# A mixture-of-experts layer on one Trainium2 core: expert rows added into a token table by scatters, in place of a result table that is gathered at the end

## What is computed

```
h  = rmsnorm(x1)                                   # h2 in the kernel
pc = softmax(h @ w_rc)       # 4 groups            -> best group g, its probability p
pf = softmax(fine logits of group g)               # 8 experts -> the best two, top_w
w  = top_w / sum(top_w) * p                        # two mixing weights per token
y  = x1 + sum over the 2 experts:  w * ((silu(h @ gate) * (h @ up)) @ w_down)
```

## Time and profile before

| | |
|---|---|
| median of 3 runs | 1653.49 us (1650.79 to 1655.81) |
| the profiled execution: its time / its span | 1649.68 / 1647.9 us |
| busy in the span: PE, DVE, ACT, POOL | 1531.3, 735.6, 398.5, 202.2 us |
| router stage | about 1048 to 1217 us |
| expert stage | 1220 to 1597 us |
| tail | 1597 to 1648 us |

### The profile page before, as it was taken

The page is one execution under the profiler, slowest core; times in us unless marked ns, Lnnn a source line. Parts: engine busy times, 40 slices in busy tenths (PEclk is TensorE's granted clock), DMA queues, the critical chain, the costliest instruction groups (busy, mean ns, idle before and its releaser), DMA issues.

```text
span 1647.9 us, 16294 instructions
## 1 busy us (share of the span) xinstructions
PE 1531.3 (93%) x6131; PEld 951.5 (58%) x6131; DVE 735.6 (45%) x1311; ACT 398.5 (24%) x662; POOL 202.2 (12%) x224
## 2 busy tenths in 40 slices
PE   8999999989987989999999999999949999999976
PEld 6676666645655657556989766555524444444432
DVE  4667876022342433797677453245433212111116
ACT  3211101015466564331313220011111111111113
POOL 0000010000000000154378200000110000000004
PEclk9999999999998999999999999999969999999997
DMA  5274873513231012325221424432368999999938
GB/s 165 80 109 138 244 231 95 139 75 83 77 89 39 25 30 91 87 68 154 75 71 29 151 67 177 158 122 102 131 201 308 368 366 374 365 369 373 365 130 309
DMA packets 232261, 273.25 MB, mean 166 GB/s; under 512 B 62516, under 2 KB 167336, under 8 KB 231920
## 3 DMA queue, kind: packets, MB, share of 16 engines
q1 hardware_dynamic: 204628, 203.54, 39.9%
q10 hardware_dynamic: 18140, 34.48, 5.5%
q0 software_dynamic: 9408, 34.08, 5.4%
HBM read 188.83 MB, written 83.24 MB: 165 GB/s over the span
## 4 chain that ended last, share of the span: by engine, by line
PE 78%; DVE 7%; ACT 6%; issue 4%; POOL 2%; DMA 2%; ACTq 0%; POOLq 0%; SPq 0%; DVEq 0%
PE P L694 24%; PE P L1143 12%; PE P L1094 7%; PE P L1050 7%; PE P L1127 6%; PE P L851 2%; PE P L875 2%; PE P L1114 2%; POOL arena L602 1%; DVE arena L1449 1%; PE P L826 1%; POOL arena L661 1%; DVE arena L1451 1%; PE P L1074 1%; PE P L720 1%
## 5 line engine op out<-in xcount | busy, mean ns | idle before, releaser
L694 PE MATMUL P<-arena 128*128 128x352 f32 (+1 forms) x1728 | 538.5, 467 | 7.8 <-ACT arena L2133 6.5
L694 PEld LDWEIGHTS P<-arena 128*128 128x128 f32 (+1 forms) x1728 | 324.5, 191 | 195.1 <-issue 37.5
L1143 PE MATMUL P<-arena 128*128 128x512 f32 x512 | 227.9, 598 | 0.8 <-ACT arena L2234 0.8
L1143 PEld LDWEIGHTS P<-arena 128*128 128x128 f32 x512 | 95.9, 192 | 110.0 <-issue 110.0
L1094 PE MATMUL P<-arena 128*128 128x512 f32 (+1 forms) x288 | 130.6, 603 | 1.9 <-DVEq L1627 1.9
L1771 DVE COPY arena<-P 128x512 f32<-128x512 f32 x32 | 22.1, 692 | 215.8 <-PE P L1114 215.8
L1050 PE MATMUL P<-arena 128*128 128x352 f32 x384 | 115.1, 459 | 1.1 <-DMA arena<-y_d 1.1
L1127 PE MATMUL P<-arena 128*128 128x512 f32 x256 | 115.3, 593 | 0.9 <-DVE arena L1811 0.9
L1050 PEld LDWEIGHTS P<-arena 128*128 128x128 f32 x384 | 72.9, 190 | 41.6 <-issue 1.2
L1094 PEld LDWEIGHTS P<-arena 128*128 128x128 f32 (+1 forms) x288 | 50.8, 183 | 63.4 <-issue 60.9
L602 POOL TENSOR_TENSOR arena<-arena,N 64x256 f32<-64x256 f32 x96 | 81.1, 845 | 49.1 <-ACT arena L2155 27.8
(11 more groups left out here) (405 smaller groups left out, 1889.4 us busy)
## 6 DMA issues: line engine op xcount, KB each, us to landing
arena<-in_w_expert_up_dram SPq DMA_DIRECT2D x32, 2048.0 KB, 12.8
arena<-in_w_expert_down_dram SPq DMA_DIRECT2D x32, 1024.0 KB, 7.4
arena<-in_w_in_dram SPq DMA_DIRECT2D x36, 512.0 KB, 4.1
x_d<-zero SPq DMA_DIRECT2D x4, 4096.0 KB, 20.2
arena<-x_d POOLq DMA_DIRECT2D x32, 512.0 KB, 5.6
y_d<-arena ACTq DMA_DIRECT2D x32, 512.0 KB, 7.7
gate_d<-arena ACTq DMA_DIRECT2D x16, 528.0 KB, 4.9
arena<-gate_d SPq DMA_DIRECT2D x24, 352.0 KB, 3.2
```

The source lines that it names most:

```text
L694: m = pe.matmul(P[0:p, b + j, 0:TBK], w[:, k, 0:p], hT[:, k, TBK * j:TBK * j + TBK], start=f, stop=l)
L1143: m = pe.matmul(P[:, i % 2, :], xgT[i % 2][:, k, :], WU[i % NWE][:, k, :], start=k == 0, stop=k == KD - 1)
```

## The change

- `y_d` goes, with the eight DMAs that clear it. In its place is `acc_d`, a DRAM table with one row for each token. SP writes `x1` of each token tile into it during the router stage.
- The mixing weights are worked out tile by tile in the router stage. `gaps` (two DVE instructions) comes behind `choose`; `exponentials` (one ACT instruction) behind the root of the next tile, with a table load to Exp ahead and one back to Sqrt behind it; `mixing_weights` (four DVE instructions) behind `h2` of the next tile.
- Before, `idx_d`, the table from slot to token, was filled only where further tiles run. Now `owner_rows` scatters a pair (token, weight) for every slot in use, 18 scatters in the router stage; ACT loads the table back once (`owners_loaded`), PE transposes it (`owners_transposed`) and DVE copies it out (`owners_of_rows`), all before the result of tile 0 is copied. Slots without a token hold 8192, which lies past the bound of the scatters, so they are skipped.
- ACT and DVE multiply by the weight `wc` as they copy the result out of PSUM. POOL then adds the rows of the tile into `acc_d` with one indirect DMA (`add_rows`) that has `compute_op=ALU.add`. A scatter waits for the one before it to land, since two tiles can hold the same token.
- In the tail SP waits for the last scatters, skips the four conditional groups, and loads nine tiles from `acc_d` into `x1`; ACT and DVE take the norm, and SP stores. The gathers, `combine`, and PE's sums are gone.

```
+        acc_d = dram("acc_d", (NT, D))
...
             for i in range(TT_):
                 n = rows(i)
                 pool.wait_ge(s_h2, i + 1)
...
+                if i >= 1:
+                    pool.wait_ge(s_mw, i)
+                    owner_rows(i - 1, pos_i, E * 128)
...
+            def add_rows(i):
+                pool.wait_ge(s_yoa, i + 1)
+                pool.wait_ge(s_yov, i + 1)
+                if i >= 1:
+                    pool.wait_ge(s_yod[(i - 1) % 2], 16 * ((i - 1) // 2 + 1))
+                pool.indirect_dma_start(acc_d, bass.IndirectOffsetOnAxis(idx_i[:, i:i + 1], 0), yo[i % 2], None,
+                                        bounds_check=NT - 1, oob_is_err=False, compute_op=ALU.add
+                                        ).then_inc(s_yod[i % 2], 16)
...
                 for i in range(lo, hi):
+                    tile_rows(i)
+                    if i == 1:
+                        pool.wait_ge(s_mw, TT_)
+                        owner_rows(TT_ - 1, pos_i, E * 128)
...
+                    if i >= lo + 4:
+                        add_rows(i - 4)
+                for i in range(hi - 4, hi):
+                    add_rows(i)
...
+            def owners_transposed(loaded):                                  # PE, behind gathered(2)
+                pe.wait_ge(s_idn, loaded)
+                bank = bank6()
+                for a in range(2):
+                    m = pe.transpose(bank[:, NTILE * a:NTILE * a + NTILE], idx_n[:, :, a], ident[0:NTILE, 0:NTILE])
+                m.then_inc(s_6, 1)
...
+            def gaps(i):                                                    # DVE
+                c = slice(i, i + 1)
+                link(dve.tensor_tensor(ex5[:, i, 0:NG], lg[:, i, :], m4[:, c].broadcast_to([128, NG]), ALU.subtract))
+                dve.tensor_tensor(ex5[:, i, NG:NG + 1], m8[1][:, c], m8[0][:, c], ALU.subtract).then_inc(s_ex, 1)
+                dve.wait_ge(s_ex, i + 1)
+
+            def mixing_weights(i):
+                c = slice(i, i + 1)
+                second = ex5[:, i, NG:NG + 1]
+                dve.wait_ge(s_exa, i + 1)
+                link(dve.tensor_reduce(p4[:, c], ex5[:, i, 0:NG], AX, ALU.add))
+                link(dve.scalar_tensor_tensor(p4[:, c], second, 1.0, p4[:, c], ALU.add, ALU.mult))
+                link(dve.reciprocal(tokw[:, i, 0, 1:2], p4[:, c]))
+                dve.tensor_tensor(tokw[:, i, 1, 1:2], tokw[:, i, 0, 1:2], second, ALU.mult).then_inc(s_mw, 1)
+                dve.wait_ge(s_mw, i + 1)
...
-                dve.tensor_copy(yo[i % 2][:, 512:1024], P[:, 3 + 2 * (i % 2), :]).then_inc(s_yov, 1)
+                dve.tensor_scalar(yo[i % 2][:, 512:1024], P[:, 3 + 2 * (i % 2), :], wc[:, i:i + 1], None,
+                                  ALU.mult).then_inc(s_yov, 1)
...
-                act.activation(yo[i % 2][:, 0:512], P[:, 2 + 2 * (i % 2), :], ACT.Copy).then_inc(s_yoa, 1)
-                act.wait_ge(s_yoa, i + 1)
-                act.wait_ge(s_yov, i + 1)
-                act.dma_start(y_d[128 * i:128 * i + 128, :], yo[i % 2]).then_inc(s_yod[i % 2], 16)
+                act.wait_ge(s_idx, 2 if i < E else 4)
+                act.activation(yo[i % 2][:, 0:512], P[:, 2 + 2 * (i % 2), :], ACT.Copy, scale=wc[:, i:i + 1]).then_inc(s_yoa, 1)
...
                 if i >= 1:
                     sp.wait_ge(s_h2, i)
                     sp.dma_start(h2_d[128 * i - 128:128 * i, :], h2[(i - 1) % 2]).then_inc(s_h2s[(i - 1) % 2], 16)
+                    sp.wait_ge(s_zid, 16)
+                    sp.dma_start(acc_d[128 * i - 128:128 * i, :], x1[:, i - 1, :]).then_inc(s_zid, 16)
...
+                for b in range(2):
+                    sp.wait_ge(s_yod[b], 16 * hi // 2)
...
+            for i in range(TT_):
+                n = rows(i)
+                sp.dma_start(x1[0:n, i, :], acc_d[128 * i:128 * i + n, :]).then_inc(s_land[i], 16)
```

More of the change, by code:

```diff
@@ L258, in hybrid_step @@
         WRr = at(q + 2048, KD, 36)
-        yg = [at(i * D, D) for i in range(2 * TT_)]
         xr = [at(q + 2336 + i * D, D) for i in range(2)]
@@ L1640, in _ @@
             link(dve.tensor_copy(tokf, tok_i[:]))
+            for j in range(2):
+                link(dve.tensor_copy(tokw[:, :, j, 0], tokf))
             link(dve.tensor_copy(tilef, des_i[:]))
```

221 lines of the change are left out of this document (88 added, 133 removed).

## The result

The changed kernel takes 1657.88 us (median of 20 runs, 1651.3 to 1661.37) against 1650.61 us (20 runs, 1647.62 to 1655.81) for the kernel before on the same chip. The ratio is 1.004, 95% interval 1.0028 to 1.0052: slower by 0.4%. The forecast was 1640 us and faster. The value lies inside the wide range of 1630 to 1670 us, which took in a rival, and outside the forecast's own of 1631 to 1647; the direction was wrong. The time base was off too: the forecast built on a median of 3 runs, 1653.49 us, which is 2.9 us above the median of 20.

What follows compares the result with a forecast made beforehand. PE was taken to bound router and expert stages, no engine the tail. 1.5 + 2.5 + 0.8 + 0 - 17.4 = -12.6 us took the profiled 1649.68 to 1637.1; predicted 1640 us, own range 1631 to 1647, wide range 1630 to 1670.

Steps and rivals of the forecast that it cites:

- Expert stage: Adding scatter in place of each tile's store: 1.2 us per engine and tile against 1.3, PE stays the bound, 0 us.
- own upper bound: Expert stage: two packets a row and all 66 rows on half the engines, 2.3 us per engine and tile.
- rival in the mild form: Expert stage: adding scatters overload the DMA engines, 20 us of PE waits, 1660 us; chance of the whole rival 0.20.
- The reserve: Expert stage: up matrices land 13.0 us after issue and are used after 22.8, so weights have some 9.8 us in hand.
- Serial scatters: Rival, expert stage: adding scatters over 10.4 us make POOL fall behind each tile; at 14 us about 1740; chance 0.08.
- Tail: From the last copy out of PSUM to the end: 33 us against 50.6, -17.4 us (bounds -24 and -8).
- Router stage and handover: Router: added DVE work stalls PE in 7 tiles, +1.5 us; handover to the experts: DVE and POOL work, +2.5 us.
- Index table: Before the expert stage: loading hidden, but PE's two transposes wait for DVE to free bank 6 and run, +0.8 us.
- Clears: The eight clears of `y_d` lie beside PE-bound projection work and are worth nothing.

Runs made afterwards that it cites:

- c_spread: The changed kernel with each expert's first 64 rows dealt to even partitions, the others to odd ones, by two more VectorE instructions a router tile; 1648.77 us, ratio 0.9978.
- c_blocks: The changed kernel with an expert's rows dealt to partitions 0 to 31, then 64 to 95, 32 to 63, 96 to 127; 1656.91 us, expert stage 372.5 us.
- c_fours: The changed kernel with an expert's first 64 rows dealt to the first four partitions of every eight, the others to the rest; 1666.84 us, expert stage 385.0 us.
- c_all128: The changed kernel with each tile's unused slots added too, into 128 spare rows of a larger table, so 128 adding rows a tile; 1648.04 us, ratio 0.9970.
- a3_clears: The changed kernel with the eight 1 MB clears put back at the same places, into a table nobody reads; 1655.43 us, ratio 1.0021.
- b_tail: The changed kernel with the tail's nine loads issued by GpSimd instead of SyncE and a buffer for each output; 1656.66 us, ratio 1.0033.
- e_ctrl: c_all128 with only the scatter's bound set so that the spare rows are skipped again; 1658.89 us, ratio 1.0064.
- a1_plain: The changed kernel with scatters that overwrite token rows instead of adding (adding left out, so no candidate); 1641.98 us, ratio 0.9936.
- a5_skipped: The changed kernel with a scatter bound that lets only token row 0 through (adding the others left out, so no candidate); 1643.46 us, ratio 0.9951.

## Why the prediction was wrong

**Expert stage, the step that failed.** "I take 1.2 (66/16 x 0.28), two packets evenly spread ... no change in demand, and PE stays the bound, 0 us". It cost +11.9 us. The price of two packets was right, 0.33 us a row against 2 x 0.16 (it is one record of twice the length). The even spread was wrong. The rows lie on half of the engines, 8 on each, so by an estimate 2.6 us of such an engine's time a tile (8 x 0.33), double the store's 1.3. c_spread, c_blocks and c_fours show it by moving rows alone. The forecast's own upper bound had 2.3 us, and its rival in the mild form 1660 us; measured were 1657.88. The mechanism of that rival is the one that came, but the nearness of its time is in part luck: it had 20 us of waits and the full gain of the tail, where 11.9 us more stage came with 5.6 us less gain. What would show it was named too: PE waits for weight loads. The forecast also knew that the used slots are the first of each tile. Against it stood only that 419 GB/s had been seen, and that is a sum over all 16 engines, which says nothing of one half of them.

**The reserve.** The rival let PE wait when the 9.8 us in hand were used up, and so it was: PE is still busy to 99.5% from 1300 to 1400 us, and most of the waits come behind that. What it did not foresee is that eight rows on every engine (c_all128) use up the reserve so much more slowly, 15.6 to 17.5 us over the stage, than eight rows on half of them. So the busiest engine's load alone does not decide, and this part stays open.

**Serial scatters.** This rival did not come about. An adding scatter of the changed kernel lands in 6.1 to 10.1 us, under the 10.4 from which GpSimd would fall behind, though over the 9 that the forecast had named; GpSimd waits for the one before only once, for 5.7 us at the last tile.

```profile
DMA to landing us min/median/max: 6.1/9.5/10.1
```

**Tail, a term that was mis-sized.** -17.4 us forecast. The mean over the changed kernel and the three others with its tail and its scatters (a3_clears 36.9, b_tail 37.0, e_ctrl 38.3) is 37.4 us, over the two profiles of before 49.2: -11.8. The part behind the first load was well forecast, 25 us against 26.0. The part ahead of it was not: "The last scatter needs 5 us ... and the one before has landed by then". The one before landed only at about 1623.9, the last started at 1624.73, 3.2 us behind E, and took some 6.4 us more. So the load went out at E + 11.5, not at E + 8. And 1.4 us of the 17.4 were in the 50.6 us of one profile.

**Router stage and handover.** +4.0 forecast, measured 180.4 against 176.2, so +4.2; over the seven profiles of the change with nothing added in that stage 178.6 to 180.6 against 174.3 and 176.2. Between profiles with the same mean granted clock in the stage the difference is as large: 180.4 against 176.2 us at 0.93, and 178.6 (a3_clears) against 174.3 at 0.94. The handover's parts were not told apart by a run. There was no drain behind a table load, as the forecast took from the earlier trace rows (changed kernel, ScalarE's timeline):

```profile
1194.91 1.28 ACT L2206 ACT_TABLE_LOAD   x1
1196.20 0.21 ACT L2206 ACTIVATE arena<-arena 128x5 f32<-128x5 f32 x1
```

**Index table.** +0.8 forecast; PE waits 0.5 us once and the two transposes take 0.4 from the first start to the last end.

**Clears.** Nothing forecast; a3_clears brings them back without a difference in time that can be told (1.0021 and 1.0040, intervals that overlap). The 8.2 us of the early part are mostly one execution's, and go with its granted clock.

**The sum.** Router +4.4 (means of the profiles named), expert stage +11.8, tail -11.8 and about +1.3 ahead give +5.7 us; the medians differ by 7.3. In place of the expert stage's 11.8, 0 was expected, and in place of -11.8, -17.4. With the rows dealt evenly c_spread's 1648.77 us are what is left, its two added instructions included.

## What to carry to other kernels

Before a store is replaced by an indirect one, ask which partitions the used rows are on, not only how many there are: with rows packed from partition 0 half of the DMA engines did all of the adding here, and a mean busy share of 0.98 hid it. Count a row that is added in DRAM as two plain ones (0.33 us against 0.16). If transfers with a deadline share the engines, deal the rows over the partitions where the slots are computed. Look at the landing time of the weights against the time between issue and use, and at the start and the end of the stage apart, since it shows the loss of reserve before any engine waits; a stage that ends in time may only have been short enough.

## What was not expected of the hardware

- Adding 62 more rows a tile, all zeros, took 11 us out of the expert stage (384.0 in e_ctrl, 373.4 in c_all128). Weight packets of 4 KB took 161 ns, where the changed kernel has 188.
- A scatter costs GpSimd 1.59 us with the add and 1.01 us without (means over 32 in the changed kernel and a1_plain); with the add the median is 1586 ns with none skipped (c_all128) and with nearly all (a5_skipped). The row is a1_plain's:

```profile
L643 POOL DMA_INDIRECT acc_d<-arena x32 | 32.4, 1013 | 137.0 <-DVE arena L1788 132.0
```

- A skipped row still sends a packet: 2199 packets under 512 B in 200 us in the changed kernel against 1120 in c_all128, where none is skipped. They are of 8 bytes and take 9 ns by the packet records.
